# Four channel groups convolved by taps on VectorE instead of three; convolution matrices read whole from memory; a new order in the last groups

## What is computed

```python
def conformer_conv_branch(h, w_in, w_dw, b_dw, g_ln, b_ln, w_o):
    a, bgl, g = jnp.split(h @ w_in, 3, axis=-1)
    u = a * jax.nn.sigmoid(bgl)
    u = lax.conv_general_dilated(u, w_dw, window_strides=(1,), padding=[(CONV_PAD, CONV_PAD)],
                                 dimension_numbers=('NWC', 'WIO', 'NWC'),
                                 feature_group_count=CONV_W) + b_dw
    u = jax.nn.silu(layer_norm(u, g_ln, b_ln)) * jax.nn.silu(g)
    return u @ w_o
```

## Time and profile before

| | us |
|---|---|
| median of 3 runs (2959.26 to 2961.14) | 2960.77 |
| the profiled execution | 2957.94 |
| its span on the core | 2956.2 |
| matmuls of `conv_in`, first to last start | 2145.8 to 2748.2 |
| busy over the whole span: PE / DVE / ACT / POOL | 2870.8 / 1982.4 / 1450.6 / 389.6 |

### The profile page before, as it was taken

How to read it: one execution, slowest core, us unless ns; L and a number is a source line. 1 busy time by engine, 2 the same in 40 slices (tenths; PEclk the granted TensorE clock), 3 DMA queues, 4 the chain that set the end, 5 groups by cost and what they waited for, 6 DMA issues and landing times. The chain is left out here.

```text
span 2956.2 us, 42917 instructions
## 1 busy us (share of the span) xinstructions
PE 2870.8 (97%) x14429; PEld 2389.1 (81%) x14429; DVE 1982.4 (67%) x3191; ACT 1450.6 (49%) x3053; POOL 389.6 (13%) x467
## 2 busy tenths in 40 slices
PE   6999999999999999999999999999999999999898
PEld 4888888778888888888888888878778888888687
DVE  6555645577767676766767677653348797987875
ACT  5554646465655565556556565544431222122643
POOL 0000000022122212221221222100000001021000
PEclk9999999999999999999999999999999999999999
DMA  7557564611211112121201111135442232323563
GB/s 272 204 199 261 182 215 162 231 53 33 76 44 54 45 60 60 33 66 44 76 26 57 60 41 49 59 118 183 148 152 79 77 96 78 99 72 118 180 200 120
DMA packets 215415, 323.65 MB, mean 109 GB/s; under 512 B 69632, under 2 KB 131344, under 8 KB 213904
## 3 DMA queue, kind: packets, MB, share of 16 engines
q1 hardware_dynamic: 210576, 312.35, 32.4%
q10 hardware_dynamic: 4608, 8.39, 0.7%
HBM read 223.03 MB, written 97.66 MB: 108 GB/s over the span
## 5 line engine op out<-in xcount | busy, mean ns | idle before, releaser
L1314 DVE TENSOR_TENSOR at_ptlo<-at_T,at_pthi 128x512 fp32r<-128x512 f32 x576 | 396.9, 690 | 304.3 <-ACT at_pthi L1192 301.4
L1176 ACT ACTIVATE at_prob<-at_S,at_nmax 128x512 f32<-128x512 f32 x634 | 407.4, 658 | 341.2 <-DVE at_nmax L1290 326.5
L1192 ACT ACTIVATE at_pthi<-at_T 128x512 fp32r<-128x512 f32 x576 | 349.0, 608 | 210.2 <-PE at_T L1058 210.2
L1279 DVE TENSOR_REDUCE at_mx<-at_S 128x1 f32<-128x512 f32 x634 | 390.5, 630 | 72.7 <-PE at_S L1031 67.2
L1058 PE MATMUL at_T<-ident,at_prob 128*128 128x128 f32 x2304 | 346.1, 273 | 4.2 <-DVE at_ptlo L1314 4.2
L1058 PEld LDWEIGHTS at_T<-ident,at_prob 128*128 128x128 f32 x2304 | 279.5, 140 | 69.5 <-DVE at_ptlo L1314 12.8
L187 PE MATMUL ci_ps<-h1hi,ci_whi 128*128 128x512 f32 x768 | 299.8, 390 | 5.3 <-DVE h1lo L2120 5.3
L188 PE MATMUL ci_ps<-h1lo,ci_whi 128*128 128x512 f32 x768 | 299.3, 390 | 0.0
L189 PE MATMUL ci_ps<-h1hi,ci_wlo 128*128 128x512 f32 x768 | 299.3, 390 | 0.0
L187 PE MATMUL at_O<-at_pthi,at_vhi 128*128 128x512 f32 x576 | 270.2, 469 | 0.6 <-DVE at_og L1328 0.5
L678 DVE TENSOR_TENSOR fr_wlo<-fr_w,fr_whi 128x1024 fp32r<-128x1024 f32 (+1 forms) x99 | 115.1, 1167 | 218.7 <-ACT fr_whi L534 218.4
(11 more groups left out here) (294 smaller groups left out, 5988.0 us busy)
## 6 DMA issues: line engine op xcount, KB each, us to landing
fr_w<-in_w_front SPq DMA_DIRECT2D x75, 512.0 KB, 4.2
at_wmod<-in_w_mod SPq DMA_DIRECT2D x32, 512.0 KB, 3.5
cv_w<-in_cv_w_in SPq DMA_DIRECT2D x24, 512.0 KB, 4.5
fr_w<-in_w_front SPq DMA_DIRECT2D x24, 384.0 KB, 4.0
values<-fr_ob SPq DMA_DIRECT2D x36, 256.0 KB, 2.8
at_vst<-values SPq DMA_DIRECT2D x8, 1152.0 KB, 7.2
fr_w_mod<-in_w_modr SPq DMA_DIRECT2D x17, 512.0 KB, 5.0
fr_x<-in_x SPq DMA_DIRECT2D x16, 512.0 KB, 6.6
```

The lines of the kernel that those rows point to most:

```text
L1176: nc.scalar.activation(prob[:, j % 2, i, k], bank(h, j, i, c)[:, 0:k.stop - k.start], ACT.Exp, scale=SCALE, bias=nmax[:, i % 2:i % 2 + 1], ...
L1192: nc.scalar.activation(dst, T[:, (n + SLOTS * j) % 2], ACT.Copy).then_inc(s_hi, 1)
L1279: nc.vector.tensor_reduce(mx[:, i % 2, c:c + 1], bank(h, j, i, c)[:, 0:k.stop - k.start], AXX, ALU.max).then_inc(s_mx, 1)
L1314: nc.vector.tensor_tensor(ptlo[:, kt % 3], T[:, (n + SLOTS * j) % 2], pthi[:, kt % 3].bitcast(F32), ALU.subtract).then_inc(s_lo, 1)
```

## The change

- `TAPPED` becomes (0, 1, 3, 4): one more group goes from the matrix engine to VectorE. BY_PE is then 2, 5, 6, 7, so chunks stand in groups 3, 6, 7 and in the tail. `TAP_RUNS` spreads the 31 taps of each group evenly over 16 steps: (0,10) to (2,1), (2,5) to (3,8), (4,0) to (5,3), (5,7) to (7,0); that is two per step, one in the first. `SUM_AT` puts the sums of the tapped groups in the 8 steps from (2,8), (4,2), (5,10) and (7,5).
- The band matrices come whole from memory (`bands`, 320 KB a chunk, three buffers). ScalarE copies the high part (`ci_bhi`, `high_parts`); VectorE subtracts it for the low part (`ci_blo`, in place of the loaded band, `low_parts`). The mask, the taps' own high and low parts and all of GpSimd's work in this stage are gone.
- The parts of chunk q+2 are made right behind chunk q: on ScalarE behind its eviction and a square, on VectorE ahead of its sums. This is about as far ahead as before.
- Two gate products of group 6 move into the tail. Its order is now G(6,2), G(7,0), chunks 0 and 1, G(7,1), chunks 2 to 4, G(6,3), chunks 5 to 7, G(7,2), G(7,3). One list `order` is the order of every engine. Loads of `conv_out`'s weights are issued one by one behind items of the tail.
- SyncE loads a band (waiting for the convolution that used its buffer three chunks before) and a chunk of u at each chunk, ahead of the store of the result.

```diff
-TAPPED = (0, 2, 4)
-TURNED_IN = (2, 4, 6)
-SUMMED_IN = (3, 5, 7)
-TAP_STEPS = [(g + a, s, n) for g in (0, 2, 4) for a, row in (
-    (1, (1, 2, 1, 2, 1, 2, 1, 2, 2, 1, 2, 1)), (2, (2, 1, 2, 1, 2, 1, 2, 1, 1))) for s, n in enumerate(row)]
+TAPPED = (0, 1, 3, 4)
+LOAD_AT = ((0, 8), (2, 2), (3, 9), (5, 4))
+TURN_AT = ((2, 3), (3, 10), (5, 5), (7, 1))
+SUM_AT = ((2, 8), (4, 2), (5, 10), (7, 5))
+TAP_RUNS = (((0, 10), (2, 1)), ((2, 5), (3, 8)), ((4, 0), (5, 3)), ((5, 7), (7, 0)))
+STEP_LIST = [(g, s) for g in range(KD) for s in range({6: 10, 7: 8}.get(g, 12))]
...
+        TAIL = ((G, L - 1, 2), (G, L, 0), (C, L, 0), (C, L, 1), (G, L, 1), (C, L, 2), (C, L, 3), (C, L, 4), (G, L - 1, 3),
+                (C, L, 5), (C, L, 6), (C, L, 7), (G, L, 2), (G, L, 3))
...
+        def parts_at(x):
+
+            kind, g, b = x
+            if kind == C:
+                return [(g, b + 2)] if b + 2 < CH else []
+            if kind == G and g in BY_PE:
+                if g == L:
+                    return [(g, 0), (g, 1)] if b == 0 else []
+                if g == L - 1:
+                    return [(g, 0), (g, 1)] if b == 1 else []
+                return [(g, b - 2)] if b >= 2 else []
+            return []
...
+            def load_band(g, q):
+                n = nth(g, q)
+                if n >= 3:
+                    sp.wait_ge(s_cv, n - 2)
+                sp.dma_start(band[:, n % 3], net.bands[g * CH + q]).then_inc(s_band[n % 3], 16)
...
+            def high_parts(g, q):
                 n = nth(g, q)
                 act.wait_ge(s_raw[q % 4], BY_PE.index(g) * 32 + 16 * (q // 4 + 1))
                 if n >= 2:
                     act.wait_ge(s_cv, n - 1)
                 nc.scalar.activation(uhi[:, q % 2, HALO:HALO + NCOL], raw[:, q % 4], ACT.Copy).then_inc(s_uhi, 1)
+                act.wait_ge(s_band[n % 3], 16 * (n // 3 + 1))
+                nc.scalar.activation(bhi[:, q % 2], band[:, n % 3], ACT.Copy).then_inc(s_bhi, 1)
...
-            def band_and_low(g, q):
+            def low_parts(g, q):
                 n = nth(g, q)
-                if n >= 2:
-                    dve.wait_ge(s_cv, n - 1)
-                nc.vector.tensor_tensor(bhi[:, q % 2], *banded(thi[:, q].bitcast(F32)), ALU.mult).then_inc(s_bhi, 1)
                 dve.wait_ge(s_uhi, n + 1)
                 nc.vector.tensor_tensor(ulo[:, q % 2, HALO:HALO + NCOL], raw[:, q % 4],
                                         uhi[:, q % 2, HALO:HALO + NCOL].bitcast(F32), ALU.subtract).then_inc(s_ulo, 1)
+                dve.wait_ge(s_bhi, n + 1)
+                nc.vector.tensor_tensor(blo[:, n % 3], band[:, n % 3], bhi[:, q % 2].bitcast(F32),
+                                        ALU.subtract).then_inc(s_blo, 1)
...
-        @block.gpsimd
-        def _(pool):
-            pool.wait_ge(s_const, CONST)
-            for p in range(len(BY_PE)):
-                pool.wait_ge(s_tlo, p + 1)
-                for q in range(CH):
-                    n = p * CH + q
-                    if n >= 2:
-                        pool.wait_ge(s_cv, n - 1)
-                    nc.gpsimd.tensor_tensor(blo[:, q % 2], *banded(tlo[:, q]), ALU.mult).then_inc(s_blo, 1)
```

More of the change, by code:

```diff
@@ new lines, in conv_in @@
+        for x in products:
+            first_tap[x] = done
+            done += taps_at.get(x, 0)
+        assert done == N_TAP
+        load_at = {step(*x): i for i, x in enumerate(LOAD_AT)}
+        turned_at = {step(g, s + e): (i, e) for i, (g, s) in enumerate(TURN_AT) for e in range(2)}
+        summed_at = {}
+        for i, x in enumerate(SUM_AT):
+            for q in range(CH):
+                summed_at[products[number[step(*x)] + q]] = (i, q)
+        reload_at = {products[number[x] - 1]: [(i, q)] + ([(i, 1)] if q == 0 else [])
+                     for x, (i, q) in summed_at.items() if q != 1}
@@ new lines, in parts_at @@
+        def parts_at(x):
[9 more added lines that the diff above has]
+            return []
+        assert sorted(y for x in order for y in parts_at(x)) == [(g, q) for g in BY_PE for q in range(CH)]
@@ L1785, in load_w, with weights_at @@
+        def weights_at(x):
+            if x == TAIL[0]:
+                return [(L, G)]
+            return [(x[1] + 1, s) for s in (B, A)] if x[0] == G and x[2] == 0 and x[1] < L else []
         def load_w(sp, g, s):
@@ new lines, in _ @@
+            for x in order:
+                kind, g, b = x
+                if kind == C:
+                    for y in parts_at(x):
+                        low_parts(*y)
+                    banded_sums(g, b)
+                    continue
+                for y in weights_at(x):
+                    w_low(*y)
+                for y in parts_at(x):
+                    low_parts(*y)
+                if g == 0 and kind != G:
+                    for y in itertools.chain(*split_behind(2 * b + kind)):
+                        h_low(y)
+                if kind != B:
+                    product(x)
+                if x == (A, g, 0) and g < L:
+                    w_low(g, G)
+                if x in summed_at:
+                    tapped_sums(*summed_at[x])
+                for n in range(first_tap[x], first_tap[x] + taps_at.get(x, 0)):
+                    tap(n)
@@ L2765, in layout @@
                     taps[:, s, j, f] = dw[t]
-    out["taps"] = taps.reshape(KD, P // CCH, P, OFFS * PHASES).transpose(0, 2, 1, 3)
+    bands = np.zeros((D // CCH, CCH, PHASES, OFFS, CCH, PHASES), np.float32)
+    for c in range(CCH):
+        bands[:, c, :, :, c] = taps.reshape(D // CCH, CCH, PHASES, OFFS, PHASES)[:, c]
+    out["bands"] = bands.reshape(D // CCH, P, OFFS * P)
     out["b_dw"] = np.repeat(a["cv_b_dw"][0].reshape(-1, CCH), PHASES, axis=1).T
```

487 lines of the change are left out of this document (192 added, 295 removed).

## The result

The changed kernel takes 2983.5 us (median of 6 runs, 2979.6 to 2985.6), the kernel before 2961.0 (6 runs, 2959.3 to 2962.5): a ratio of 1.0077, with a 95% interval of 1.0067 to 1.0087. It is **slower by 22.6 us**. The forecast was slower by 15, 2976 us; the time lies in its range. The profiled execution after has a span of 2982.0 us against 2956.2.

The account below looks back on a forecast made before the run. It took TensorE's list as the bound of `conv_in`, longer where VectorE is late. New waits 32.4 and the end 1.9, less 14.2 and 5.8, gave +14.3 us on 2960.8, put at 2976 us; range 2955 to 2992.

Parts of the forecast that it names:

- stretch two: Groups 5 and 6, up to the parts of group 5's chunk 7: VectorE late, 14.9 us of new TensorE waits.
- eight chunks fewer, old waits gone: TensorE's forty chunks become 32, saving 14.2 us, and its 5.8 us of old waits for VectorE's `ci_ulo` go.
- stretch one: Groups 2 and 3, from product (2,7) to the parts of chunk 6: VectorE late, 8.2 us of new TensorE waits.
- group 7's weights: Before step (7,0) TensorE waits for VectorE's sums, taps, product and `ci_wlo`: 2.4 us.
- chunk 0 of group 6: After (7,0) VectorE needs 7.8 us up to this chunk's parts against one step of 5.4: 2.3 us wait.
- tail: Chunks 2, 3, 4 and 5, 6, 7 follow without a product: TensorE waits 2.3 us twice, 4.6 us.
- end: Behind the last matmul, now of a gate product, come sigmoid, product and store: 1 to 2 us longer, say 1.9.
- the eight turns: Turns of a tapped row, which every first tap waits for: taken at 13.0 us for 8.
- VectorE keeps pace: Rival: VectorE's average load decides, so the kernel gets faster, 2947 us; chance 0.12.
- Only stretch two, half of it: Rival: only groups 5 and 6 are late, by half the figure; about 2958 us, no change; chance 0.08.
- SyncE's list: Rival: band loads stand behind late stores in SyncE's single list, some 1 us for each of 16 chunks; 2991 us; chance 0.08.
- the tail's crowded DMAs: Small losses in the tail, for which the forecast was put at 2976 us instead of 2975.1.

Follow-up runs that it names:

- e4: The changed kernel with the tail in its old order, everything computed: 2981.9 us, ratio 1.0072 to the kernel before.
- e5: The kernel before, with only idle additions on VectorE ahead of two of TensorE's 1.75 us waits: 2970.9 us, ratio 1.0037 to the kernel before.
- e2: The changed kernel with most taps of two tapped groups (1 and 4) run over half the columns, result incomplete: 2947.9 us, ratio 0.9958 to the kernel before.
- e3: The changed kernel with three tapped groups (0, 2, 4), their taps, turns and sums placed as before the change: 2958.7 us, ratio 0.9994 to the kernel before.
- e6: The changed kernel with the same work, but the times of taps, loads, turns and sums moved: 2968.8 us, ratio 1.0035 to the kernel before.
- e8: The changed kernel run and profiled once more with no edit: 2982.2 us, ratio 1.0076 to the kernel before.

## Why the prediction was right, and by how much it was short

**The direction and the mechanism** were right: VectorE's average load (472 us of the 585 from 2160 to 2745, 81%) did not decide, the two stretches did. That the sum came so near is in part luck, as the paragraph on stretch two below shows. Step by step, from the timeline of after:

| term | forecast | measured |
|---|---|---|
| eight chunks fewer, old waits gone | -14.2 - 5.8 | -14.2 (120 matmuls fewer, at the same price) - 5.8 |
| stretch one | 8.2 | 2.65 + 2.48 + 1.40 + 1.39 = 7.9 |
| stretch two | 14.9 | 4.19 + 5.41 + 1.40 + 1.68 + 1.40 + 1.68 = 15.8 |
| group 7's weights | 2.4 | 2.1 |
| chunk 0 of group 6 | 2.3 | 2.1 |
| tail | 4.6 | 1.92 + 1.78 = 3.7 |
| end | 1.9 | 1.6 |
| clock behind the waits | not in the sum | 7.2 |
| refill at ten waits more | not in the sum | 2.5 |

The waits sum to 31.6 us against 32.4. In stretch one, which starts where VectorE is not behind, adding up VectorE's instructions at undisturbed durations and taking TensorE's work away was good: from the product of (2,7) to the end of chunk 6's `ci_blo` VectorE took 78.9 us against 78.1 + 0.55. The prices held: `ci_blo`, which no row of before showed and which I put at 0.82, took 0.82; ScalarE's copy, put at 0.7, took 0.725; and the taps no longer stretch beside GpSimd. The longest tap was 3.379 us before and is 2.355 now (tile views of after, then of before; duration ns min/median/max):

```profile
L2123 DVE TENSOR_TENSOR ci_blo<-ci_band,ci_bhi x32: 816/820/826, 2346.5 to 2759.3; 128x640 fp32r<-128x640 f32 x32
L1980 ACT ACTIVATE ci_bhi<-ci_band x32: 719/725/750, 2336.8 to 2758.6; 128x640 fp32r<-128x640 f32 x32
L2086 DVE SCALAR_TENSOR_TENSOR ci_acc<-ci_ut,ci_tap_w,ci_acc x120: 2323/2351/2355, 2217.7 to 2675.2; 128x2048 f32<-128x2048 f32 x120
```

```profile
L2074 DVE SCALAR_TENSOR_TENSOR ci_acc<-ci_ut,ci_tap_w,ci_acc x90: 2324/2346/3379, 2225.8 to 2640.3; 128x2048 f32<-128x2048 f32 x90
```

**Stretch two** came out right by two errors that met. I had the product of (5,8) about 7 us behind TensorE; it was twice that (timelines of ACT, DVE and PE, after):

```profile
2432.79 1.32 ACT L1999 ACTIVATE ci_zr<-ci_acc 128x256 f32<-128x256 f32 x2 [2.42 <-DVE ci_acc L2086]
2442.39 1.26 ACT L1999 ACTIVATE ci_zr<-ci_acc 128x256 f32<-128x256 f32 x2 [8.28 <-DMA z_phases<-ci_zr]
...
2450.38 1.35 DVE L2083 TENSOR_SCALAR ci_acc<-ci_ut,ci_tap_w,ci_tap_b 128x2048 f32<-128x2048 f32 x1 [5.05 <-ACT ci_zr L1999]
...
2549.02 0.39 PE L199 MATMUL ci_ps<-h1hi,ci_wlo 128*128 128x512 f32 x1
...
2563.00 1.09 DVE L2069 TENSOR_TENSOR ci_ub<-ci_ps,ci_sig 128x512 f32<-128x512 f32 x1
```

The step that was mis-sized is the eight turns, which I took over at 13.0 us. They took 17.6 us here (2432.79 to 2450.38), and 15.3 the next time (2544.15 to 2559.47): nearly 7 us more in the two. ScalarE waited 8.28 and 7.25 us for the first stores of turned rows to land, where it had waited 3.72 at the turns of rows 6. In both cases SyncE had issued the next row's load of 1 MB 1.2 to 1.5 us ahead of the first of these stores, and that store landed in 6.6 and 6.9 us; in before the load was issued 9 us ahead, and the store landed in 3.0. (That the load is the reason is read from this order; no run moves the load alone.) From the product of (5,8) on VectorE took the 80.2 us that I had counted (78.8 and the waits for squares). TensorE needed 94.3 us from (5,8) to chunk 7 against my 72.3. Only 15.8 of the 22.0 us of lateness stand as waits. The other 6 went, but for 0.7, into TensorE's own slower pace: 9.2 us of matmuls at 1.2 GHz, which lose 4.0, and six refills, 1.5. I had left both out, and the one error hid the other.

**Slips in the working.** The terms of the lateness at (5,8) add up to 6.4, not 7. The five times of the tail's path add up to 2.8 us, not 3.9, and 3.9 - 1.78 is 2.1, not 2.3; the two waits measured were 1.92 and 1.78. The stretches hold 15 preparations of a chunk (7 + 8), not 13, so the 14 us named for GpSimd's part would have been 16.5. None of these turns the forecast.

**The end** has the right size, and in this kernel the right reason. The last matmul starts at 2772.79. The product ends at 2774.95, and its store is issued at 2774.97 and lands 2.8 us later; the next stage's first instructions start 1.3 us behind that, at 2779.04. Before, the last sum ended at 2751.80 and the next stage began 1.0 us later. What I had not seen is that the old order would not have helped: in e4 the last store is that of a chunk again and its end is no shorter (+1.8). That store landed in 4.1 us, against 1.7 for the last one in before. A load of 512 KB for `conv_out` had been issued 1.3 us ahead of it, where in before the last such load was issued 12 us ahead. That the load caused the delay is read from the order in SyncE's list, and no run tests it.

**What was short** is the sum line itself: "New waits 32.4, the end 1.9; away go 14.2 ... and 5.8" takes a wait at the length of its row. It left out 7.2 us of clock and 2.5 of refills, 9.7 us in all, against which the waits and the end were 0.8 + 0.3 too dear. That gives 14.3 + 9.7 - 1.1 = 22.9, with 22.6 measured. The clock term is shown by e5, where only VectorE was given more to do; the refill term is worked out from starts and stands at every wait, but no run tests it alone. I did have the pattern at hand: the stage's first matmuls, behind the 5.3 us for `h1lo`, ran at half the clock for 3 us in before. The Trainium skill (TensorE: Matmul & The Clock Gate, "What's actually happening") says that the slow clock is the state of rest and that activity lifts it; the runs agree for the long waits and leave the short ones undecided.

**The rivals.** *VectorE keeps pace*, 2947 us, is what e2 looks like (2947.9) once two groups' taps are halved: the price of that rival was right and its condition was not met. *Only stretch two, half of it* falls: both stretches were late by the full figure. *SyncE's list*, as late bands, falls by e2 and e3; ScalarE waited for bands 5.4 us in six times, at most 1.7 at once. By another way SyncE's list did count: through the stores of the turns, as told above. The small 1 us put on for "the tail's crowded DMAs" has nothing behind it either.

Can four tapped groups pay at all? Not in a spacing tried here. e6 removed 12.7 us of waits and needs another 9. e3 shows that the rest of the change (the bands from memory, with the new tail) neither gains nor costs measurably with three groups: 0.9994 (0.9985 to 1.0004). No kernel that computes the whole result came out measurably faster than the one before.

## What to carry to other kernels

Where two engines are near each other in load, cut the program at the places where the busier one is certainly not behind, and sum both engines' instructions between the cuts; here the average over the stage did not decide. Where no such place can be had, as in stretch two, the lateness at the start is a term of its own, and each wait for a store in it is to be priced by what SyncE issues just ahead of that store. When the sum leaves TensorE waiting several us, add to each wait the time that its next matmuls lose at half the clock and a quarter of a us for the refill: here that was four tenths of the net loss. And when a step is moved, count what it waits for, not only what it does, since all that stands behind it in the same queue waits too.

## What the runs showed that I had not expected

- TensorE's granted clock fell to 1.2 GHz in a stage where it is busy 95 to 99% of the time, at single waits of 1.8 to 7.0 us, for 3.4 us or twice that, and matmuls of 128x256 stood 0.213 us apart instead of 0.119.
- The fall slows TensorE just when it is waiting for another engine, so some of it comes back as shorter waits later: after and e8 share the waits (31.6 and 27.7 us) and the clock (7.2 and 10.7) out differently and take the same time. In stretch two of after 6 us of VectorE's lateness vanished in this way.
- A store that was issued 1.2 to 1.5 us behind a load of 512 KB to 1 MB took 4.1 to 6.9 us to land, against 1.7 to 3.0 for the like ones in before. The two rounds of turns that had such a store were 2.3 and 4.6 us longer.
- `co_all`, the first matmul behind the stage, waits 6.5 to 6.8 us in the eight kernels built on the new code and 4.9 in the two built on the old (before and e5), whatever the order of the tail. In the three that were looked at (before, after and e4) the next stage begins 1.0 to 1.3 us behind the last thing of `conv_in`: a sum in before, the landing of a store in the others.
